# Return of the experts tile by tile, with the norm's weights and bias applied after the transposes

## The reference, cut to what matters

```
for l in range(2):                       # first stack
    y = mixer(x, ...)
    x = layer_norm(ALPHA * x + y, ln1_g[l], ln1_b[l])
    y = moe(x, router_w, router_b, ...)  # 16 experts in 4 groups, 2 experts per row
    x = layer_norm(ALPHA * x + y, ln2_g[l], ln2_b[l])

layer_norm(x, g, b) = (x - mean) * rsqrt(var + 1e-5) * g + b

for l in range(2):                       # second stack: feed-forward, mixer, feed-forward
    h = rms_norm(x, norm_pre[l, 0])      # its scale per row is applied behind the first product
    ...
```

## Time and profile before

| | us |
|---|---|
| median of 3 runs | 2383.14 (2381.06 to 2383.84) |
| the profiled execution's own time | 2383.86 |
| its span in the trace | 2382.3 |
| TensorE busy | 2298.4 (96%) |
| VectorE busy | 1755.2 (74%) |
| ScalarE busy | 1409.6 (59%) |
| mean granted TensorE clock | 0.994 |

### The profile page before, as it was taken

How to read it: one execution, slowest core, us unless ns; L and a number is a source line. 1 busy time by engine, 2 the same in 40 slices (tenths; PEclk the granted TensorE clock), 3 DMA queues, 4 the chain that set the end, 5 groups by cost and what they waited for, 6 DMA issues and landing times.

```text
span 2382.3 us, 39448 instructions
## 1 busy us (share of the span) xinstructions
PE 2298.4 (96%) x11114; PEld 1875.9 (79%) x11114; DVE 1755.2 (74%) x2348; ACT 1409.6 (59%) x1892; POOL 236.9 (10%) x296
## 2 busy tenths in 40 slices
PE   9998999999998999999999999999999999989998
PEld 7777788878777788877887867888878877778887
DVE  6778888887778888897556788765565568887555
ACT  5653777774653777774446576454464466765445
POOL 0000000000000000000000692000000008800000
PEclk9999999999999999999999999999999999999999
DMA  7444899985444799995555544565656554455652
GB/s 263 129 144 133 303 340 332 345 326 160 151 135 152 277 336 335 342 333 191 185 185 177 163 140 150 186 205 185 193 188 186 184 179 141 156 170 161 211 184 97
DMA packets 277777, 497.33 MB, mean 209 GB/s; under 512 B 20512, under 2 KB 112848, under 8 KB 277632
## 3 DMA queue, kind: packets, MB, share of 16 engines
q1 hardware_dynamic: 273440, 481.60, 60.6%
q0 software_dynamic: 4192, 14.02, 2.0%
HBM read 494.50 MB, written 1.05 MB: 208 GB/s over the span
## 4 chain that ended last, share of the span: by engine, by line
PE 69%; DVE 14%; DVEq 6%; issue 4%; ACT 3%; DMA 1%; ACTq 1%; PEldq 0%; SPq 0%; PEld 0%; POOLq 0%
PE g_bank L625 14%; PE g_bank L626 13%; PE g_bank L627 13%; PE s_bank L627 8%; PE s_bank L625 8%; PE s_bank L626 8%; DVE w_lo L598 4%; DVE conv_y L2700 2%; DVEq L2694 1%; PE t_bank L1783 1%; DVEq L2304 1%; ACT w_hi L593 1%; PE t_bank L1943 1%; DVE row_max L2328 1%; PE t_bank L1807 0%
## 5 line engine op out<-in xcount | busy, mean ns | idle before, releaser
L598 DVE TENSOR_TENSOR w_lo<-w_raw,w_hi 128x1024 fp32r<-128x1024 f32 x909 | 1095.7, 1235 | 337.0 <-ACT w_hi L593 312.2
L593 ACT ACTIVATE w_hi<-w_raw 128x1024 fp32r<-128x1024 f32 x909 | 944.5, 1058 | 408.1 <-PE g_bank L627 170.3
L625 PE MATMUL g_bank<-w_hi,xt_hi 128*128 128x512 f32 (+1 forms) x1136 | 453.8, 399 | 11.5 <-ACT gate L1401 5.1
L626 PE MATMUL g_bank<-w_lo,xt_hi 128*128 128x512 f32 (+1 forms) x1136 | 442.6, 390 | 0.0
L627 PE MATMUL g_bank<-w_hi,xt_lo 128*128 128x512 f32 (+1 forms) x1136 | 442.4, 389 | 0.0
L625 PEld LDWEIGHTS g_bank<-w_hi,xt_hi 128*128 128x128 f32 x1136 | 215.6, 190 | 67.0 <-issue 13.4
L627 PEld LDWEIGHTS g_bank<-w_hi,xt_lo 128*128 128x128 f32 x1136 | 215.2, 189 | 45.3
L626 PEld LDWEIGHTS g_bank<-w_lo,xt_hi 128*128 128x128 f32 x1136 | 215.6, 190 | 40.3
L625 PE MATMUL s_bank<-w_hi,xt_hi 128*128 128x512 f32 x608 | 240.2, 395 | 0.0
L627 PE MATMUL s_bank<-w_hi,xt_lo 128*128 128x512 f32 x608 | 237.3, 390 | 0.0
L626 PE MATMUL s_bank<-w_lo,xt_hi 128*128 128x512 f32 x608 | 236.9, 390 | 0.0
(11 more groups left out here) (366 smaller groups left out, 2887.2 us busy)
## 6 DMA issues: line engine op xcount, KB each, us to landing
w_raw<-in_w_in_dram SPq DMA_DIRECT2D x192, 512.0 KB, 4.6
w_raw<-in_moe_w_gate_dram SPq DMA_DIRECT2D x128, 512.0 KB, 5.3
w_raw<-in_moe_w_up_dram SPq DMA_DIRECT2D x128, 512.0 KB, 5.6
w_raw<-in_moe_w_down_dram SPq DMA_DIRECT2D x128, 512.0 KB, 5.3
w_raw<-in_ffn_w_gate_dram SPq DMA_DIRECT2D x176, 256.0 KB, 2.9
w_raw<-in_ffn_w_up_dram SPq DMA_DIRECT2D x176, 256.0 KB, 3.1
w_raw<-in_ffn_w_down_dram SPq DMA_DIRECT2D x88, 512.0 KB, 3.4
w_raw<-in_w_branch_dram SPq DMA_DIRECT2D x40, 512.0 KB, 4.4
```

Of the source, the lines that this page charges most:

```text
L593: nc.scalar.activation(half_of(w_hi, u, h), half_of(w_raw, u, h), ACT.Copy).then_inc(hi_ready, 1)
L598: nc.vector.tensor_tensor(half_of(w_lo, u, h), half_of(w_raw, u, h), half_of(w_hi, u, h).bitcast(F32), ALU.subtract).then_inc(lo_ready, 1)
L625: nc.tensor.matmul(dst, a_hi, b_hi, start=first, stop=False)
L626: nc.tensor.matmul(dst, a_hi, b_lo, start=False, stop=False)
```

## The change

1. The return's order: for tile 0 groups 0 to 2, then group 3, then the same for tile 1. VectorE makes tile 0's statistics and variance between the adds, with a semaphore of its own.
2. VectorE writes only (acc - mean) * rstd, in place into acc, as a tensor_scalar with two per-partition scalars. That is transposed. ScalarE reads the transposed bank with four Identity activations of 128 x 128, whose scale and bias are per-partition columns (gain_col), into xt_full, then copies that to xt_hi; VectorE makes xt_lo from xt_full.
3. gain_col, the norm's weights and bias with one number per partition and block of 128, is loaded by GpSimd with a non-contiguous pattern; at the end of the first stack it is multiplied by first_col, the next norm's weights. VectorE waits for all of gains before the experts.
4. x itself (x_res) is made after all that from acc by four pairs of VectorE passes, with the broadcast gains and bias.
5. Of the held halves only half 1 is split under the return; halves 2, 3 and 4 are split between the steps of the norm. So each round of experts starts with halves 2 and 3, and half 4 is split after the first gather, no longer around the router.
6. The idle products: 54 and 8 become 12 and 16, 64 becomes 12 and 16.

The core of the diff, without the declarations and without VectorE's splits of halves 1 to 4, which move as ScalarE's do:

```diff
                 for i, w in enumerate(("ln2_g", "ln2_b")):
                     pool.dma_start(gains[:, i, :], d[w][bass.ds(l, 1), :].to_broadcast([P, DM])).then_inc(gains_in, 16)
+                    pool.dma_start(gain_col[:, i, :], d[w][bass.ds(l, 1), :].rearrange("a (k p) -> p (a k)", p=P), allow_slow_non_contiguous=True).then_inc(gains_in, 16)
                 if stacks == 2 and l == DEPTH - 1:
-                    pool.dma_start(first_gain[:, :], d["norm_pre_2"][0:1, 0, :].to_broadcast([P, DM])).then_inc(pre_in, 16)
+                    pool.dma_start(first_col[:, :], d["norm_pre_2"][0:1, 0, :].rearrange("a (k p) -> p (a k)", p=P), allow_slow_non_contiguous=True).then_inc(pre_in, 16)
@@ ScalarE, experts() @@
-                    for place in held:
-                        ahead(place)
-
+                        if what == "gather" and part == "start":
+                            split_hi(at_r["u"], 4)
+                    if held:
+                        split_hi(held[0], AHEAD)
+
+                for h in range(2, 4):
+                    split_hi(at_r["u"], h)
                 all_parts(act, run)
@@ ScalarE, before the router and after it @@
-                for h in range(2, 4):
-                    split_hi(u + 30, h)
...
-                split_hi(u + 30, 4)
@@ ScalarE, behind the experts @@
-                for tt in range(TT):
-                    tile_root(tt, At(2 + tt, (l, 4)))
-                    if l < DEPTH - 1:
-                        act_xt(layer1(l + 1, done)["t"] + 2 * tt, 2, TILE[tt])
-                    elif stacks == 2:
-                        act_xt(layer2(0, done)[0]["t"] + 2 * tt, 2, TILE[tt])
+                def affine(tt, kq):
+                    tf = t_next + (2 * tt + kq)
+                    act.wait_ge(t_ready, tf.value(1, 1))
+                    for j in range(4):
+                        k = 4 * kq + j
+                        last = act.activation(xt_full[:, tt, kq, j * P:(j + 1) * P], t_bank[tf.slot(2)][:, j * P:(j + 1) * P], ACT.Identity,
+                                              scale=gain_col[:, 0, k:k + 1], bias=gain_col[:, 1, k:k + 1])
+                    last.then_inc(t_free[tf.slot(2)], 1)
+                    act.drain()
+                    act.activation(xt_hi[:, 4 * kq:4 * kq + 4, tt * P:(tt + 1) * P],
+                                   xt_full[:, tt, kq, :].rearrange("p (a b) -> p a b", a=4), ACT.Copy).then_inc(xt_hi_ready, 1)
+
+                act.activation(root_of[:, :], c("ones", 0, 1), ACT.Sqrt)
+                act.wait_ge(first_var_ready, done)
+                act.activation(rstd[:, 0:1], rstd[:, 0:1], ACT.Sqrt).then_inc(rstd_ready, 1)
+                act.wait_ge(cols_ready, l + 1)
+                affine(0, 0)
+                tile_root(1, At(3, (l, 4)))
+                split_hi(u_next, 2)
+                affine(0, 1)
+                split_hi(u_next, 3)
+                affine(1, 0)
+                affine(1, 1)
+                split_hi(u_next, 4)
@@ TensorE @@
-                    x_quads(t, 8 * l, 0, 54)
+                    x_quads(t, 8 * l, 0, 12, acc)
...
-                        idle_products(bank, 8 if l else 24)
+                        idle_products(bank, 16 if l else 24)
...
-                    for groups in (range(NG - 1), (NG - 1,)):
+                    for tt, groups in ((0, range(NG - 1)), (0, (NG - 1,)), (1, range(NG - 1)), (1, (NG - 1,))):
                         pe.wait_ge(y_ready, 4 * rnd + (groups[-1] + 1))
-                        for i in range(4):
-                            tt, nb = i // 2, i % 2
+                        for nb in range(2):
+                            i = 2 * tt + nb
...
-                        idle_products(t_wait(t), 64)
+                        idle_products(t_wait(t), 12)
...
+                        if l + i + tt == 0:
+                            idle_products(bank, 16)
@@ VectorE, before the experts @@
+                dve.wait_ge(gains_in, 96 * l + 96)
+                if l == DEPTH - 1 and stacks == 2:
+                    dve.wait_ge(pre_in, 16)
+                    dve.tensor_tensor(gain_col[:, :, :], gain_col[:, :, :], first_col[:, :].unsqueeze(1).to_broadcast([P, 2, 8]), ALU.mult)
+                dve.drain().then_inc(cols_ready, 1)
                 R = rounds_loop(dve, 1, l + 1)
@@ VectorE, the return @@
                         dve.tensor_tensor(a_, a_, g_bank[b][:, :], ALU.add).then_inc(g_free[b], 1)
+                        if tt == 0:
+                            row_stats(acc, 0, nb)
+                        if i == 1:
+                            variance(0).then_inc(first_var_ready, 1)
...
+                def normed(tt):
+                    dve.drain()
+                    dve.wait_ge(rstd_ready, At(2 + tt, (l, 4)).value(1, 1))
+                    for kq in range(2):
+                        a_ = acc[:, tt, kq * 512:(kq + 1) * 512]
+                        dve.tensor_scalar(a_, a_, mean_var[:, tt, 0:1], rstd[:, tt:tt + 1], ALU.subtract, ALU.mult).then_inc(row_sem, 1)
...
+                dve.sem_inc(var_ready, 1)
+                normed(0)
+                for nb in range(2):
+                    row_stats(acc, 1, nb)
+                variance(1).then_inc(var_ready, 1)
+                affine_lo(0, 0)
+                normed(1)
+                split_lo(u_next, 2)
+                affine_lo(0, 1)
+                split_lo(u_next, 3)
+                affine_lo(1, 0)
+                affine_lo(1, 1)
+                split_lo(u_next, 4)
                 for tt in range(TT):
-                    for nb in range(2):
-                        row_stats(acc, tt, nb)
-                    if tt and (stacks == 2 or l < DEPTH - 1):
-                        dve_xt(t_next, n_next, 2, TILE[0], each=True)
-                    norm_first(acc, x, tt, gain, 64 * l + 64)
-                    for kq in range(2):
-                        norm_second(x, tt, At(2 + tt, (l, 4)), bias, (kq,))
-                        if l == DEPTH - 1 and stacks == 2:
-                            norm_in(ffn_y, 0, 0, tt, kq, first_gain)
-                    if tt:
-                        dve.drain().then_inc(x_ready, 1)
-                if stacks == 2 or l < DEPTH - 1:
-                    dve_xt(t_next + 2, n_next + 2, 2, TILE[1], each=True)
+                    for gain_row, op in ((gain, ALU.mult), (bias, ALU.add)):
+                        dve.drain()
+                        for kq in range(2):
+                            cols = slice(kq * 512, (kq + 1) * 512)
+                            dve.tensor_tensor(x[:, tt, cols], (acc if op == ALU.mult else x)[:, tt, cols], gain_row[:, cols], op)
+                dve.drain().then_inc(x_ready, 1)
```

More of the change, by code:

```diff
@@ L462, in build @@
         acc = sb("acc", [P, TT, DM], scope=moe)
-        first_gain = sb("first_gain", [P, DM], scope=moe)
+        xt_full = sb("xt_full", [P, TT, 2, 512], scope=moe)
+        gain_col = sb("gain_col", [P, 2, 8], scope=moe)
+        first_col = sb("first_col", [P, 8], scope=moe)
         moe.close()
@@ L1207, in _ @@
                 done = act.snap(rho, min_val=0, max_val=4)
[L1208 to L1213 removed]
+                if l < DEPTH - 1:
+                    u_next, t_next = layer1(l + 1, done)["u"], layer1(l + 1, done)["t"]
+                elif stacks == 2:
+                    u_next, t_next = layer2(0, done)[0]["u"], layer2(0, done)[0]["t"]
+                def affine(tt, kq):
[21 more added lines that the diff above has]
+                split_hi(u_next, 4)
             if stacks < 2:
@@ L1536, in idle_products, with x_quads @@
                     pe.transpose(bank[:, 0:P], ident, ident)
-            def x_quads(t, rows_before, tt, idle=0):
+            def x_quads(t, rows_before, tt, idle=0, src=x):
                 for kq in range(2):
@@ L1545, in x_quads @@
                     for j in range(4):
-                        last = pe.transpose(bank[:, j * P:(j + 1) * P], x[:, tt, (4 * kq + j) * P:(4 * kq + j + 1) * P], ident)
+                        last = pe.transpose(bank[:, j * P:(j + 1) * P], src[:, tt, (4 * kq + j) * P:(4 * kq + j + 1) * P], ident)
                     last.then_inc(t_ready, 1)
@@ L2391, in _ @@
                             dve_xt(t + (T_AFTER_MIX1 + 4), At(12, (l, 16)), 2, TILE[0])
-                    norm_first(x, x, tt, gains[:, 0, :], 64 * l + 32, times=2)
+                    norm_first(x, x, tt, gains[:, 0, :], 96 * l + 32, times=2)
                     norm_second(x, tt, At(tt, (l, 4)), gains[:, 1, :])
@@ L2395, in _ @@
                 dve_xt(t + (T_AFTER_MIX1 + 6), At(14, (l, 16)), 2, TILE[1])
-                for h in range(2, 4):
-                    split_lo(u + 30, h)
                 tf = t + (T_AFTER_MIX1 + 8)
@@ L2471, in combination, with variance @@
                     dve.drain().then_inc(comb_ready, 1)
+                def variance(tt):
+                    dve.drain()
+                    dve.bn_aggr(mean_var[:, tt, :], stats[:, tt, :])
+                    dve.drain()
```

(30 more changed lines are left out.)

9 lines of the change are left out of this document (4 added, 5 removed).

## The result

| | us |
|---|---|
| kernel before, median of 20 runs | 2381.36 (2378.97 to 2383.84) |
| changed kernel, median of 20 runs | 2386.41 (2384.73 to 2387.24) |
| ratio | 1.002, 95% interval 1.0014 to 1.0026 |
| changed kernel's profiled execution | 2386.86 (span 2385.2) |

The change makes the kernel 5.05 us slower. The forecast was 2.3 us slower, in a range of 2379 to 2390: the sign and the main mechanism held, but half of the size was missing. The page's chain of work that ended last, by engine, answers to the earlier trace rows and shows only that a little more of it is TensorE's and ScalarE's; the stretches tell where.

What follows compares the result with a forecast made beforehand. TensorE, busy in 96% of the span, was taken as the bound, so only stretches without real products could give time; 0 + 3.7 + 0.5 - 1.9 = +2.3 on the median of 2383.14 gave 2385.4 us, range 2379 to 2390.

Steps and rivals of the forecast that it cites:

- Part 1: From a layer's return to the next first real product: it comes 4.4 us earlier, at 548.55.
- Part 2: Inside the block behind the return: TensorE waits 0.7 and 1.7 us, so 2.15 of the 4.4 us are left.
- Part 3, second layer: Start of the second stack: x made later delays squares, splits and hidden tile; TensorE waits 6.8 us for half 5; +3.7 us.
- term of 0.5 for the low clock: Start of the second stack: 0.5 us added for low clock after the 6.8 us wait, the rest covered by the hidden tile.
- Part 3, first layer: First layer's half 5: x made later makes TensorE wait 2.1 us, set against the earlier block; 0 us in sum.
- rival D: Slower: TensorE falls to 1.2 GHz after the waits of 2.1 and 6.8 us, uncovered, 1.6 us each; 2388.6 us; chance 0.15.
- Part 4: Start of the experts in both layers: splits leave the router's path, first product 0.95 us earlier each, -1.9 us.
- B: Faster: x made later isn't in the way of half 5 or the hidden tile; 9.2 us less, 2374; chance 0.11.
- C: Slower: gain_col's columns land late and VectorE holds back splits and xg_lo, 12 us in sum; 2397; chance 0.10.

Runs made afterwards that it cites:

- order_only: The kernel before with only the return's order changed to tile by tile; 2381.0 us, ratio 0.9999.
- after: The changed kernel itself, with the whole change and nothing added; median 2386.41 us, profiled execution 2386.86 us.
- experts_warm: The changed kernel with 12 idle products between the gather and the experts' first product; 2385.52 us, ratio 1.0019.
- cols_three: The changed kernel with each load of gain_col made three times, into places of their own; 2385.76 us, ratio 1.0019.
- x_twice_first: The changed kernel with the eight passes for x made twice in the first layer only; 2394.76 us, ratio 1.0055.
- second_warm: The changed kernel with 54 idle products in front of half 5 at the start of the second stack; 2386.75 us, ratio 1.0022.
- silu_first: x_early with, at the second stack's start, halves 5 and 6 split before x's squares, silu and hidden tile before halves 7 and 8; 2376.31 us, ratio 0.9975.
- both_warm: silu_first with the 12 idle products of experts_warm before the experts' first product; 2374.39 us, ratio 0.9968.
- x_early: The changed kernel with x's passes moved into VectorE's idle time, only the last pair staying behind half 4's split; 2378.94 us, ratio 0.9991.
- held_back: The changed kernel with halves 1 to 4 split under the return again and the experts' halves around the router; 2390.26 us, ratio 1.0038.
- before_silu_first: The kernel before with only silu_first's reorder at the start of the second stack; 2381.81 us, ratio 1.0002.

## Why the prediction was right and where it was not

**Part 1** (first product 4.4 us earlier): 549.52 less the 0.40 us by which this execution's return began later is 549.1, 3.9 us earlier than before; predicted 548.55. The gap without real products fell from 10.0 and 11.3 to 6.1 and 5.7 us, where some 5.5 was predicted. The normalising pass took 1.00 us for two of 512 columns, near my 0.45 each, and VectorE sat 0.85 us before it, where I had taken 0.4. The four affine pieces took 1.50 us; by my 86 ns for each per-partition operand it was 1.49. The Trainium skill (ScalarE: Activation LUTs, "What ACT_TABLE_LOAD costs") gives such an operand 93 ns, by which the same working is an estimate of 1.54: the trace agrees with it as well. Order_only shows what the prediction left unsaid: the order gains nothing by itself.

**Part 2** (waits of 0.7 and 1.7): TensorE waited 0 and 1.27 us.

**Part 3, second layer** (x in the way, +3.7, and 0.5 for the clock): right. Wait 6.8 us predicted, 6.81 measured; squares +4.6 predicted, +4.84 measured (0.48 of it brought along); return 2 is 3.8 us longer (48.5 as the mean of after, experts_warm, cols_three, x_twice_first; 44.75 of before and order_only), against 4.2. The term of 0.5 for the low clock is too small for second_warm to settle (return 2 0.5 shorter than that mean, the median 0.3 longer).

**Part 3, first layer** (0): wrong by 0.4 to 2.0 us. The wait was 2.02 us as predicted. But I held that against the gain in front of it and took the sum for the whole: behind a wait of 2.0 us the clock fell in two of four executions (return 1 of 42.99 and 42.98, against 41.41 and 41.42). I had priced that in rival D, with 1.6; it is 1.57, in half of these executions.

**Part 4** (-0.95 each): this is the step that failed. Without a fall of the clock, start 1 is 0.73 us shorter (28.88 against 29.60) and start 2 0.1 on the mean (215.3 against 215.4). I counted when the products could start, not how long TensorE idled before: the wait grew to 2.25 and 2.6 us, behind which the clock fell in six of twelve cases, for 1.4 to 1.6 us each. On the mean (29.7 and 216.0) the starts brought 0 and +0.6 us instead of -1.9. Why start 2 gained so little even without a fall is open. There VectorE multiplies gain_col by first_col ahead of its splits, a step the prediction gave no time, and the first of them starts 2.62 us behind the gather instead of 2.24 (776.83 to 779.45, 234.39 to 236.63); no run tests whether that is the cause.

The sum by these means is 3.8 + 1.25 (return 1: 42.2 against 40.95) + 0 + 0.6 = 5.65 us, against 5.05 measured; the remainder is within what single profiles scatter. That is 3.35 us more than the forecast. The low clocks behind waits of 2.0 to 2.6 us make about 2.3 of it (half of 1.57, 1.55 and 1.4), the starts' smaller gain without a fall 1.1, half 5's own lateness 0.5, and the second layer takes 0.4 back. This division rests on counting falls in single profiles; of the medians only the step from silu_first to both_warm speaks for it. The upper end of the range, 2389, also lies above what the prediction's own terms give, 2385.4 + 2.4 = 2387.8.

**Rivals.** B (x not in the way) fell: x_early is 7.5 us faster. C (columns late) fell with cols_three. D had the mechanism but one wrong place: not in the second stack, where the low clock is covered, but at the first layer's half 5 and at the two starts of the experts, where the prediction had no loss at all.

## What to carry to other kernels

Splitting an operation so that its first user gets what it needs sooner leaves a remainder; look for its other readers before placing it. Here the remainder (x) was put at the end of the queue, ahead of a chain of seven steps, while VectorE had idle time of 3.05 and 1.41 us a few lines earlier in its own timeline. And when a wait of TensorE is moved or lengthened, price not only the wait but the clock behind it.

## What the runs showed that I had not expected

The granted clock behind a wait is not a fixed cost. The same waits of 2.0 to 2.6 us were followed by the low clock in 8 of 16 cases; behind the waits of 1.64 us at the experts' starts (before, order_only, held_back, before_silu_first) it fell in none of 8, and behind those of 0.9 to 1.3 in none of 4. A fall cost 1.4 to 1.6 us. The length of the last wait is not all that counts: at the second layer's return of the kernel before, where idle products, transposes and a wait of 0.97 us stand in front of the last wait, the granted clock was down behind 1.72 us in before and behind 1.74 in order_only, and up behind 1.72 in before_silu_first, whose code there is the same:

```profile
1096.00:1100.00 4.00, 3.71 (x16) 3.08 (x17) 3.35 (x9) 0.20 (x1) 0.00 (x0) 1.00 0.00 0
```

A median over many runs sees the mean of such falls, and a single profile all or nothing; so a gain of 1.6 us per place in one trace promised more than the runs of experts_warm, 0.9 us in all, show.
